# Moving operands shifted by 32 bytes, and another order of the three products of a weight tile

## The reference

```python
def layer_forward(x, p_i, norm_g, w1g, w1u, w1d, w2g, w2u, w2d, w_pe, w_pg, mix):
    x = x + 0.5 * swiglu(rmsnorm(x, norm_g[0]), w1g, w1u, w1d)      # 1024 -> 2816 -> 1024
    y, st = mix(rmsnorm(x, norm_g[1]))      # layer 0: attention, layer 1: recurrent block
    x = x + y
    x = x + 0.5 * swiglu(rmsnorm(x, norm_g[2]), w2g, w2u, w2d)
    x = x + (p_i @ w_pe) * jax.nn.sigmoid(rmsnorm(x, norm_g[3]) @ w_pg)
    return x, st
```

## Time and profile before

| | |
|---|---|
| runs | 1204.94, 1205.96, 1206.43 us |
| the profiled execution's own time | 1206.72 us |
| its span, first to last instruction | 1204.6 us |
| instructions in the span | 23286 |
| products of three matmuls | 2820, that is 8460 matmuls of 288 or 292 columns out of 8952 |
| mean granted TensorE clock | 0.993 of full speed |

### The profile page before, as it was taken

One profiled execution on the slowest core, in us unless ns is written; L12 is line 12 of the kernel. 1 busy time (PEld: TensorE's weight loads), 2 busy tenths in 40 slices (PEclk: granted clock), 3 DMA queues, 4 the chain that ended last, 5 costly groups with the idle time before them and its releaser, 6 DMA issues.

```text
span 1204.6 us, 23286 instructions
## 1 busy us (share of the span) xinstructions
PE 1178.3 (98%) x8952; PEld 1168.4 (97%) x8952; DVE 795.4 (66%) x1170; ACT 584.4 (49%) x862; POOL 170.3 (14%) x201
## 2 busy tenths in 40 slices
PE   6999999999999999999999999999999999999996
PEld 6999999999989999999999999999999999999995
DVE  7666555677758665565785566456989856655566
ACT  6444433466645444343564444335695544443353
POOL 3000002211123000011230000021306300000222
PEclk9999999999999999999999999999999999999998
DMA  6544444743335445444455444446453554544542
GB/s 211 198 147 168 153 147 166 257 138 121 106 114 200 154 170 174 140 146 165 157 196 175 153 161 152 150 163 187 134 189 113 195 180 156 174 153 143 170 152 87
DMA packets 37627, 193.19 MB, mean 160 GB/s; under 512 B 4001, under 2 KB 6321, under 8 KB 26049
## 3 DMA queue, kind: packets, MB, share of 16 engines
q1 hardware_dynamic: 36528, 187.86, 46.5%
q0 software_dynamic: 1040, 4.51, 1.1%
HBM read 188.78 MB, written 3.58 MB: 160 GB/s over the span
## 4 chain that ended last, share of the span: by engine, by line
PE 90%; DVE 5%; ACT 3%; issue 1%; DMA 1%; SPq 0%; DVEq 0%; ACTq 0%
PE bank L1154 30%; PE bank L1156 29%; PE bank L1155 29%; DVE w_lo L784 2%; ACT w_hi L513 1%; DVE conv L908 1%; DMA raw<-in_up 1%; PE bank L1185 0%; DVE u_ext L921 0%; PE bank L1169 0%; DVE stay L849 0%; DVE logit L841 0%; DVE conv L937 0%; ACT stay L555 0%; ACT stay L552 0%
## 5 line engine op out<-in xcount | busy, mean ns | idle before, releaser
L513 ACT ACTIVATE w_hi<-raw 128x1024 fp32r<-128x1024 f32 (+2 forms) x410 | 370.4, 927 | 341.0 <-PE bank L1156 327.0
L784 DVE TENSOR_TENSOR w_lo<-raw,w_hi 128x1024 fp32r<-128x1024 f32 (+2 forms) x410 | 457.5, 1134 | 85.5 <-ACT w_hi L513 82.6
L1154 PE MATMUL bank<-xg_hi,w_hi 128*128 128x288 f32 x1536 | 458.8, 299 | 9.3 <-DVE w_lo L815 8.3
L1155 PE MATMUL bank<-xg_lo,w_hi 128*128 128x288 f32 x1536 | 454.5, 296 | 0.0
L1156 PE MATMUL bank<-xg_hi,w_lo 128*128 128x288 f32 x1536 | 453.0, 295 | 0.0
L1154 PEld LDWEIGHTS bank<-xg_hi,w_hi 128*128 128x128 f32 x1536 | 289.0, 188 | 11.2 <-issue 8.0
L1156 PEld LDWEIGHTS bank<-xg_hi,w_lo 128*128 128x128 f32 x1536 | 290.5, 189 | 0.0
L1155 PEld LDWEIGHTS bank<-xg_lo,w_hi 128*128 128x128 f32 x1536 | 289.7, 189 | 0.4
L1154 PE MATMUL bank<-h_hi,w_hi 128*128 128x288 f32 x704 | 208.4, 296 | 0.0
L1155 PE MATMUL bank<-h_lo,w_hi 128*128 128x288 f32 x704 | 207.7, 295 | 0.0
L1156 PE MATMUL bank<-h_hi,w_lo 128*128 128x288 f32 x704 | 207.0, 294 | 0.0
(11 more groups left out here) (185 smaller groups left out, 1246.2 us busy)
## 6 DMA issues: line engine op xcount, KB each, us to landing
raw<-in_up SPq DMA_DIRECT2D x85, 1024.0 KB, 4.9
raw<-in_down SPq DMA_DIRECT2D x64, 704.0 KB, 4.0
raw<-in_qkv SPq DMA_DIRECT2D x24, 512.0 KB, 4.6
raw<-in_ple SPq DMA_DIRECT2D x16, 640.0 KB, 3.9
raw<-in_lru_in SPq DMA_DIRECT2D x12, 512.0 KB, 4.8
raw<-in_lru_o SPq DMA_DIRECT2D x8, 640.0 KB, 3.9
raw<-in_wo SPq DMA_DIRECT2D x4, 1024.0 KB, 5.3
raw<-in_lru_g SPq DMA_DIRECT2D x8, 512.0 KB, 4.4
```

Source lines behind the costliest of these rows:

```text
L513: nc.scalar.activation(w_hi[slot][:, cols], raw[slot][:, cols], ACT.Copy).then_inc(w_hi_done, 1)
L784: nc.vector.tensor_tensor(w_lo[slot][:, cols], raw[slot][:, cols], w_hi[slot][:, cols].bitcast(F32), ALU.subtract).then_inc(w_lo_done, 1)
L1154: nc.tensor.matmul(out, w_hi[slot][:, cols], hi[:, k, 0:width], start=start, stop=False)
L1155: nc.tensor.matmul(out, w_hi[slot][:, cols], lo[:, k, 0:width], start=False, stop=False)
```

## The change

A helper, activations, declares a tensor of 16 columns (64 bytes) more and uses it from column 8 on, so that its data begin 32 bytes past a multiple of 64. xg, xg_side, h, o and y go through it, and gate_g, which shares y_lo's room, is shifted with it. p was 32 bytes past one before; it and the weights, 128 bytes further on now, keep their place against a multiple of 64. c keeps its turning chunks. product writes the low weight x high activation second and the high weight x low activation third. No instruction is added or removed.

```diff
         x = sb("x_res", [P, KD, TOK])
-        xg_main = (sb("xg_hi", [P, KD, TOK], F32R), sb("xg_lo", [P, KD, TOK], F32R))
+        def activations(name, chunks, scope):
+
+            return sb(name, [P, 16 + chunks * TOK], F32R, scope)[:, 8:8 + chunks * TOK] \
+                .rearrange("p (k t) -> p k t", k=chunks)
+
+
+        xg_main = (activations("xg_hi", KD, ctx), activations("xg_lo", KD, ctx))
...
-            h_hi = sb("h_hi", [P, KF, TOK], F32R, scope)
-            h_lo = sb("h_lo", [P, KF, TOK], F32R, scope)
-            xg_side = (sb("xg_side_hi", [P, KD, TOK], F32R, scope), sb("xg_side_lo", [P, KD, TOK], F32R, scope))
+            h_hi = activations("h_hi", KF, scope)
+            h_lo = activations("h_lo", KF, scope)
+            xg_side = (activations("xg_side_hi", KD, scope), activations("xg_side_lo", KD, scope))
...
-            o_hi = sb("o_hi", [P, KD, TOK], F32R, scope)
-            o_lo = sb("o_lo", [P, KD, TOK], F32R, scope)
+            o_hi = activations("o_hi", KD, scope)
+            o_lo = activations("o_lo", KD, scope)
...
-            y_hi = sb("y_hi", [P, KR, TOK], F32R, scope)
+            y_hi = activations("y_hi", KR, scope)
             with ExitStack() as inner:
-                gate_g = sb("gate_g", [P, KR, TOK], F32, inner)
-            y_lo = sb("y_lo", [P, KR, TOK], F32R, scope)
+                gate_g = sb("gate_g", [P, 16 + KR * TOK], F32, inner)[:, 8:8 + KR * TOK] \
+                    .rearrange("p (k t) -> p k t", k=KR)
+            y_lo = activations("y_lo", KR, scope)
...
                 nc.tensor.matmul(out, w_hi[slot][:, cols], hi[:, k, 0:width], start=start, stop=False)
-                nc.tensor.matmul(out, w_hi[slot][:, cols], lo[:, k, 0:width], start=False, stop=False)
-                return nc.tensor.matmul(out, w_lo[slot][:, cols], hi[:, k, 0:width], start=False, stop=stop)
+                nc.tensor.matmul(out, w_lo[slot][:, cols], hi[:, k, 0:width], start=False, stop=False)
+                return nc.tensor.matmul(out, w_hi[slot][:, cols], lo[:, k, 0:width], start=False, stop=stop)
```

## The result

The changed kernel takes 1198.44 us (median of 4 runs, 1197.36 to 1200.05), the kernel before 1206.01 us in the same measurement: a ratio of 0.9941, 95% interval [0.9928, 0.9954]. It is faster by 0.6%; 1188.8 us, 1.4%, was forecast. The profiled execution took 1197.61 us, 9.1 us less than that of before.

The account below looks back on a forecast made before the run. PE's matmul pitch, 133.3 ns, was taken as the bound. 1206.72 us profiled less 17.1 (7335 matmuls x 2.33 ns) gave 1189.6, or 1188.8 us against the median; own range 1181.8 to 1200.8, full range 1163 to 1209 us.

Parts of the forecast that it names:

- What bounds the kernel: Whole kernel: PE, busy 98% of the span, sets the time as a count of matmuls times their 133.3 ns pitch.
- The nine tenths: Of about 8150 affected matmuls 7335 were counted, since for a tenth of the span the chain runs through other engines.
- The 32-byte shift: Product matmuls: pitch falls 2.3 ns to 131.0 ns, read from p in the first embedding gate; 17.1 us gained.
- no change: Rival, 22%: pitch returns to 133.3 ns whatever the address, six p matmuls being too few for a steady state; 1206 us.
- The bounds: Recorded durations of p, p_lo and y_lo bound the gain per matmul: 0.7 ns low, 4 to 5 ns high.
- c as a second witness: c's durations at four places stand 1.7 ns above h's, just its four more columns; so a small effect.
- The order: The new order of a tile's three products adds nothing: no load saved or added, no wait moved.
- The slower rival: Rival, 16%: low weight x high activation keeps 3 ns more on 2717 matmuls, 8.2 us lost, 1214.1 us.
- The writers: ScalarE and VectorE writing 32 bytes off: 8 ns per instruction, covered by matmuls; uncovered, about 1.4 us at 176 chunks.
- One pitch in all phases: All phases get the same places, so a pitch differing between phases would make the prediction wrong in kind.
- The rule that spoke against it: Two independent PE read ports, PE never waiting: an operand's place against the weights could not matter; 1206 us.
- estimate of 122.5 ns: Pitch of an undisturbed 288-column matmul by N / 2.4 + 2.5 ns, near 1126 us; the prediction did not use it.

Follow-up runs that it names:

- run 5: The changed kernel with tensors 256 instead of 64 bytes longer, so all operands lie at p's places, 32 and 160: 1210.91 us, ratio 1.003.
- run 13: The changed kernel with high activations from column 16, low ones from column 0, both at 64 and 192 bytes: 1198.44 us, ratio 0.9935.
- run 2: The kernel before with the new order of products alone, operands unshifted: 1206.41 us, ratio 1.000.
- run 4: The changed kernel with chunks 1280 instead of 1152 bytes apart, high activations all at place 160, low ones at 224: 1196.10 us, ratio 0.9917.
- run 15: The changed kernel with chunks 1280 bytes apart and all activations 16 bytes past a multiple of 256: 1191.31 us, ratio 0.9881.
- run 12: The changed kernel with column 8 set back to column 0, the padding kept: 1206.01 us, ratio 1.000.
- run 16: The changed kernel with the weights also used from byte 32 of buffers 256 bytes longer: 1207.20 us, ratio 1.0002.

## Why the prediction was right and wrong, point by point

**What bounds the kernel: right.** PE's pitch sets the time; its waits did not change, and 8150 x 1.11 ns = 9.0 us is the whole difference of the two profiled executions. The nine tenths that the sum allowed for the chain's other engines would give 8.1; the medians differ by 7.6, the profiles by 9.1. The nine tenths were not the step that failed.

**The 32-byte shift: the step that failed.** "The 0.07 us, divided by the 30, is 2.3 ns for each p matmul: a pitch of 131.0 ns." The difference of 0.07 us was real; that p's place made it was not. At p's places long streams settle at 133.3 or 134.4 ns (run 5), none below the aligned ones. And in run 5 xg has the same two places as p, yet 150 matmuls of which 30 are on p are again 0.07 us shorter than 150 on xg alone:

```profile
399.55 0.30 PE L1161 MATMUL bank<-xg_hi,w_hi 128*128 128x288 f32 x1
...
419.72 0.30 PE L1161 MATMUL bank<-xg_hi,w_hi 128*128 128x288 f32 x1
...
593.61 0.29 PE L1161 MATMUL bank<-p_hi,w_hi 128*128 128x288 f32 x1
...
613.71 0.29 PE L1161 MATMUL bank<-p_hi,w_hi 128*128 128x288 f32 x1
```

20.17 and 20.10 us. So the 0.07 us needs no other place; what is left is the passing from one operand to the other and back, which saves nothing in the changed kernel (19.84 us against 19.83). Six matmuls on p are such a passage, not a state. By the starts in the kernel before, only 9 of the 13 ns by which a group of 30 is shorter lie on its six p matmuls; 4 lie on the nine xg matmuls behind them.

Nor did p lie "as the change wants them all": the prediction looked at the distance to a multiple of 64 alone. Of the changed kernel's places p shares those of the high activations; the low ones lie 64 bytes further on, and runs 5 and 13 show that this matters and that the distance to a multiple of 64 does not decide. So p was no sample of the changed kernel, not even by sign. The measured term is 1.11 ns in place of 2.33; which trait of the pattern of places gives it, the runs do not isolate. The rival "no change" had named the weakness, six matmuls in a row, and drew the wrong conclusion from it.

**The bounds: wrong in kind.** The 0.7, 4 and 5 ns came from recorded durations, which stayed at 295.0 ns in mean for h while the pitch fell. Starts were the only witness. That the measured 1198.44 us still lies within the forecast's own 1181.8 to 1200.8 is luck, since its low end, 0.7 ns, is one of these durations.

**c as a second witness: luck.** It spoke for a small effect, but it was read from durations too, and "just the columns" is not what the starts say: c's pitch in the kernel before, two waits left out, is 133.8 ns, 0.5 above h's and not 1.7.

**The order: right.** Costed at nothing, and it costs nothing (run 2). The slower rival, which hung on it, did not happen, and starts speak against it: in the first h of the changed kernel the mean distance to the next start is 131.6 ns behind a low weight x high activation and 132.5 and 132.6 ns behind the other two.

**The writers: right that they cost nothing, wrong in size.** Not 8 ns: the 16 xg_lo whose chunk is taken from a loop register take 1117 ns (last section) instead of the 641 of the kernel before. VectorE has the room: PE's waits are what they were. The chunks of xg, xg_side and h are 152, not 176, which changes little.

**One pitch in all phases: right here, wrong as a rule.** The prediction took it that the same places must give the same pitch. In the changed kernel they do; in run 4 the same places give 131.1 and 132.2 ns, in run 15 130.0 and 131.7.

**The rule that spoke against it.** The p rows disagreed with "PE and ACT never wait on anyone" only by the faulty reading. Run 12, the changed kernel and run 16 are the sound witness: with the same instructions and nearly the same waits they have 133.3, 132.2 and 133.3 ns by place alone. By the rule of the Trainium skill (SBUF — State Buffer, "Who interferes with whom") they should not differ. The estimate of 122.5 ns from the Trainium skill (TensorE: Matmul & The Clock Gate, "Back-to-back issue gap"), where it is the gap of an isolated matmul, was not reached; the lowest steady pitch of any run is 130.0 ns.

**What stays open.** Which of the two reads is held up, by what, and which pattern of places gives which pitch. That the weight load and the moving stream hinder each other fits all runs, and run 16 shows that the weights' place matters; the hindrance itself no record shows. Work of VectorE and ScalarE is no rival: in the kernel before, stretches of twelve xg matmuls in the first window take 133.33 ns a matmul with VectorE busy for over nine tenths of them and with it idle for over nine tenths, and the same holds for ScalarE. DMA traffic was not parted off. What picks one of several steady pitches was not tried.

## What to carry to other kernels

Where long runs of matmuls, each with its own weights, are the bound, try the places of moving operands against weights as a parameter and measure whole streams, in more than one execution. Do not read a steady rate from a short passage between other streams, nor from recorded matmul durations; take starts, over hundreds of matmuls, at the very places in question. A gain that comes with a layout may be another layout's loss: here 1191 us and 1214 us differ by nothing but where the activations lie, so when a tensor is added or padded, the place should be looked at again.

## What the runs showed of the hardware that was not expected

- With the same instructions at full clock, the pitch of a 288-column matmul with its own weight load is 130.0 to 135.6 ns by place alone; 120 ns would be one column a cycle at 2.4 GHz.
- A stream settles on one of a few values, in many cases 3.33 ns apart in the triple, and keeps it for a whole phase; the same program can settle on another in another execution (130.0 and 131.7 ns).
- A VectorE instruction can be slower only because the tensor of one of its operands is used from an offset. The groups on xg_lo, mean ns: the second in the kernel before, and both in the run with padding and no shift (run 12):

```profile
L793 DVE SCALAR_TENSOR_TENSOR xg_lo<-x_res,vecs_sb,xg_hi x16 | 10.3, 641 | 15.2 <-ACT xg_hi L518 15.2
...
L800 DVE SCALAR_TENSOR_TENSOR xg_lo<-x_res,vecs_sb,xg_hi 128x288 fp32r<-128x288 f32 x40 | 30.1, 773 | 16.1 <-ACT xg_hi L525 16.1
L800 DVE SCALAR_TENSOR_TENSOR xg_lo<-x_res,vecs_sb,xg_hi x16 | 9.6, 599 | 15.2 <-ACT xg_hi L525 15.2
```

and in the changed kernel, where only the 16 whose chunk comes from a loop register have changed:

```profile
L800 DVE SCALAR_TENSOR_TENSOR xg_lo<-x_res,vecs_sb,xg_hi 128x288 fp32r<-128x288 f32 x40 | 29.5, 756 | 16.6 <-ACT xg_hi L525 16.5
L800 DVE SCALAR_TENSOR_TENSOR xg_lo<-x_res,vecs_sb,xg_hi x16 | 17.9, 1117 | 16.2 <-ACT xg_hi L525 16.2
```

It is not a matter of a multiple of 64: in run 13 both operands are on one, only xg_hi is used from an offset, and the 16 take 1116 ns. Why was not tried.
